# Expert products of a mixture-of-experts stage: sample rows and prompt rows alternated within each feature tile

## The reference, cut to what matters

```python
def expert_choice_ffn(h, w_router, w_gate, w_up, w_down):
    cap = EC_FACTOR * n // N_EXPERTS
    aff = jax.nn.softmax((xt @ w_router).astype(jnp.float32), axis=-1)
    gate, idx = lax.top_k(aff.T, cap)
    xe = jnp.take(xt, idx, axis=0)
    hid = jax.nn.silu(jnp.einsum('ecd,edf->ecf', xe, w_gate)) * jnp.einsum('ecd,edf->ecf', xe, w_up)
    ye = jnp.einsum('ecf,efd->ecd', hid, w_down) * gate[..., None].astype(h.dtype)
```

## Time and profile before

| | |
|---|---|
| median of three runs | 3492.0 us |
| the profiled execution's own time | 3490.68 us |
| its span, first to last instruction | 3488.8 us |
| mean granted TensorE clock | 0.988 of full speed |
| TensorE busy (matmul) | 3366.9 us, 97% |
| VectorE, ScalarE, GpSimd busy | 1302.6, 707.1, 158.1 us |
| DMA traffic | 675.69 MB, mean 194 GB/s |

### The profile page before, as it was taken

How to read it: one execution, slowest core, us unless ns; L and a number is a source line. 1 busy time by engine, 2 the same in 40 slices (tenths; PEclk the granted TensorE clock), 3 DMA queues, 4 the chain that set the end, 5 groups by cost and what they waited for, 6 DMA issues and landing times.

```text
span 3488.8 us, 47739 instructions
## 1 busy us (share of the span) xinstructions
PE 3366.9 (97%) x20879; PEld 1891.6 (54%) x20879; DVE 1302.6 (37%) x2509; ACT 707.1 (20%) x1538; POOL 158.1 (5%) x179
## 2 busy tenths in 40 slices
PE   6999999999999899999989999999999998999998
PEld 4547766765554544434355577677655545444333
DVE  3455443437543311212143544433375423211113
ACT  3131111115332300000021311111153322000001
POOL 1000000000100000000100000000001000000000
PEclk9999999999999899999999999999999999999999
DMA  7343242332232699999952423324412417999997
GB/s 221 103 114 84 66 125 64 103 94 91 81 142 88 227 380 391 396 385 390 385 153 77 134 64 98 93 64 103 109 75 81 165 64 287 383 396 390 395 386 300
DMA packets 218049, 675.69 MB, mean 194 GB/s; under 512 B 9779, under 2 KB 22297, under 8 KB 214257
## 3 DMA queue, kind: packets, MB, share of 16 engines
q1 hardware_dynamic: 198096, 613.97, 49.8%
q0 software_dynamic: 13312, 43.05, 4.8%
q10 hardware_dynamic: 6432, 15.62, 1.2%
HBM read 605.91 MB, written 66.68 MB: 193 GB/s over the span
## 4 chain that ended last, share of the span: by engine, by line
PE 90%; DMA 5%; ACT 3%; DVE 2%; issue 1%; ACTq 0%; DVEq 0%; POOLq 0%
PE unit L842 12%; PE unit L1354 11%; PE unit L790 11%; PE work L1357 9%; PE work L1354 6%; PE unit L854 4%; PE unit L833 3%; PE unit L1226 3%; PE unit L873 3%; PE unit L784 3%; DMA ring<-in_w_e_gate 2%; PE unit L1179 2%; PE work L1044 2%; PE work L1078 2%; PE unit L800 1%; PE work L1144 1%
## 5 line engine op out<-in xcount | busy, mean ns | idle before, releaser
L842 PE MATMUL unit<-hT,ring 128*128 128x512 f32 x1024 | 475.5, 593 | 0.0
L1354 PE MATMUL unit<-ring,arena 128*64 128x512 f32 x1568 | 354.7, 597 | 4.7 <-DMA ring<-in_w_e_gate 3.3
L1357 PE MATMUL work<-ring,arena 128*32 128x256 f32 x4608 | 274.8, 382 | 0.0
L2316 DVE SCALAR_TENSOR_TENSOR arena<-work,arena 32x256 f32<-32x256 f32 x128 | 61.6, 482 | 552.2 <-PE work L1357 550.8
L842 PEld LDWEIGHTS unit<-hT,ring 128*128 128x128 f32 x1024 | 177.9, 191 | 140.6 <-issue 140.6
L1354 PEld LDWEIGHTS unit<-ring,arena 128*64 128x64 f32 x1568 | 109.4, 137 | 225.6 <-issue 214.6
L1357 PEld LDWEIGHTS work<-ring,arena 128*32 128x32 f32 x4608 | 136.8, 109 | 159.5 <-issue 80.6
L790 PE MATMUL unit<-hT,ring 128*128 128x512 f32 x512 | 221.1, 592 | 0.0
L1839 ACT ACTIVATE arena<-work 128x512 f32<-128x512 f32 x32 | 19.1, 597 | 850.0 <-PE work L1371 850.0
L1354 PE MATMUL work<-ring,arena 128*64 128x512 f32 x736 | 166.6, 594 | 2.4 <-ACT arena L1840 2.1
L790 PE MATMUL unit<-arena,ring 128*128 128x512 f32 x384 | 166.8, 592 | 0.0
(11 more groups left out here) (447 smaller groups left out, 4717.6 us busy)
## 6 DMA issues: line engine op xcount, KB each, us to landing
ring<-in_w_e_gate SPq DMA_DIRECT2D x50, 2048.0 KB, 15.1
ring<-in_w_e_up SPq DMA_DIRECT2D x48, 2048.0 KB, 14.2
ring<-in_w_e_down SPq DMA_DIRECT2D x46, 2048.0 KB, 15.7
ring<-in_w_in SPq DMA_DIRECT2D x32, 2048.0 KB, 15.8
ring<-in_w_ada SPq DMA_DIRECT2D x24, 2048.0 KB, 8.8
arena<-in_w_e_down SPq DMA_DIRECT2D x18, 2048.0 KB, 14.9
arena<-in_w_e_up SPq DMA_DIRECT2D x16, 2048.0 KB, 13.7
arena<-in_w_e_gate SPq DMA_DIRECT2D x14, 2048.0 KB, 16.3
```

Of the source, the lines that this page charges most:

```text
L842: last = mm(bank[:, :], w[:, k, m * P:(m + 1) * P], hT[:, k, 0:TS], start=k == 0, stop=k == KD - 1)
L1354: last = mm(big[SLS * c:SLS * c + SLS, :], x, w[:, kk, 512 * c:512 * c + 512], start=k == 0, stop=k == KD - 1)
L1357: last = mm(low[SLOTP * c:SLOTP * c + SLOTP, 0:256], xp, w[:, kk, 256 * c:256 * c + 256], start=k == 0, stop=k == KD - 1)
```

## The change

In five of an expert's six chunks (all but d1) the two runs are gone. Within each feature tile the order is now: the narrow products of quarters 2 and 3, the wide product of half 0, the narrow products of quarters 0 and 1, the wide product of half 1. Chunk d1 keeps a narrow run and then a wide run, as before. Products, operands, banks, waits and the counting of `moe_computed` are the same.

```diff
-                    for wide in ((True, False) if half == 0 else (False, True)):
+
+                    def product(kk, wide, c):
+                        k = 4 * half + kk
+                        if wide:
+                            x = hidT[:, kk, half, :] if kind == "d" else XE[e % 2][:, k, 0:SLS]
+                            return mm(big[SLS * c:SLS * c + SLS, :], x, w[:, kk, 512 * c:512 * c + 512],
+                                      start=k == 0, stop=k == KD - 1)
+                        x = hidTp[:, k % 2, k // 2, :] if kind == "d" else XE[e % 2][:, k, SLS:SLS + SLOTP]
+                        return mm(low[SLOTP * c:SLOTP * c + SLOTP, 0:256], x, w[:, kk, 256 * c:256 * c + 256],
+                                  start=k == 0, stop=k == KD - 1)
+
+                    if part == "d1":
                         for kk in range(4):
...
+                            for c in range(4):
+                                last = product(kk, False, c)
+                        last.then_inc(sig["moe_computed"], 1)
+                        for kk in range(4):
+                            for c in range(2):
+                                last = product(kk, True, c)
+                    else:
+                        for kk in range(4):
+                            for c in range(2):
+                                product(kk, False, 2 - 2 * c)
+                                product(kk, False, 3 - 2 * c)
+                                last = product(kk, True, c)
                     last.then_inc(sig["moe_computed"], 1)
```

More of the change, by code:

```diff
@@ L1346, in expert_chunk @@
                         pe.wait_ge(sig["slots_ready"], 3 * l + 3)
-                    for wide in ((True, False) if half == 0 else (False, True)):
-                        for kk in range(4):
[L1349 to L1360, removed]
+                    def product(kk, wide, c):
[7 more added lines that the diff above has]
+                                  start=k == 0, stop=k == KD - 1)
```

## The result

The changed kernel takes 4628.57 us, the median of 4 runs (4627.2 to 4629.84), against 3492.37 before (4 runs, 3490.94 to 3495.26): a ratio of 1.3253 with a 95% interval of 1.3237 to 1.3268. It is slower by 1136 us. The forecast was 4650, range 4520 to 4780.

The account below looks back on a forecast made before the run. The TensorE was taken to bound the kernel, with DMA close behind. An expert period 36.55 us longer, 32 times, gives 1170 us; less 10 for waits, on 3490.7, that is 4651, stated as 4650, range 4520 to 4780.

Parts of the forecast that it names:

- The column kinds don't share the array: On the TensorE, halves and quarters never stream together; a change of kind drains the array. Forecast chance 0.91, 4650 us.
- The stretches: In each mixed chunk, narrow stretches take 0.57 us and wide ones 1.01, a pair 1.58, a chunk 12.64.
- The edge terms: At stretch edges on the TensorE: entering and leaving cost 0.03 and 0.11 us for narrow, 0.05 and 0.10 for wide.
- Edge price: Cost of a change between halves and quarters on the TensorE: 0.14 us a narrow stretch, 0.15 a wide one.
- The upper bound from the small products of rows 8: Edge costs of 0.22 and 0.19 us, from products of 16 streamed columns, would add 154 us: 4805 us.
- The lower bound: If a stretch's first weights load while the other kind streams, entering costs vanish, 102 us less: 4550 us.
- What else moves: In the expert stages, fewer waits for weights and less backlog take 10 us off, between 4 and 20.
- part of the backlog: Some of the backlog at the end of the first expert stage goes, within the 10 us taken off.
- The rival of the falling clock: With half of the columns idle, the clock drops to 1.2 GHz for half of both expert stages: 5770 us, chance 0.02.
- The rival of strictly ordered starts: In mixed chunks, TensorE passes start strictly in program order without a drain: period 58.5 us, 4285 us, chance 0.02.
- The rival of the shared array: In mixed chunks, halves and quarters stream together, and DMA limits the gain: 3455 to 3490 us, say 3475, chance 0.05.
- The 25 us allowed for layer 1: Most that layer 1's expert stage could shrink if DMA rose from 377 to 395 GB/s.

Follow-up runs that it names:

- e1: The changed kernel's mixed order with each wide product of 64 rows issued as two quarter products of 32 rows: 3493.64 us, ratio 1.0002 to the kernel before.
- e4: The changed kernel, but each mixed chunk runs quarters 2 and 3 for all four feature tiles, then half 0, quarters 0 and 1, half 1: 4367.35 us.
- e7: The kernel before, wide products cut into two quarter products, and three of four expert chunks loading three of four feature tiles: 3459.07 us, ratio 0.9905.
- e6: The kernel before, with three of four expert chunks loading only three of their four feature tiles: 3481.47 us, ratio 0.9974.
- e5: The kernel before, with the wide run doing all four feature tiles of half 0 first, then all of half 1: 3670.41 us.
- e2: The kernel before, runs kept, with each wide product issued as two quarter products of 32 rows: 3495.59 us, ratio 1.0011.

## Why the prediction was right

- **The column kinds don't share the array.** This was the step on which all hung, read from the half that lay idle in rows 6 and 7. It held: the changed kernel's timeline shows it, e1 shows that the kind and nothing else in the order is the cause, and e4 that longer runs don't change it. It was read from a single place in the router's part, and e1 is the run that excludes another cause of the wait there.
- **The stretches.** 0.57 and 1.01 were forecast, 0.56 and 1.00 measured. A chunk takes 12.47 us (1299.74 to 1312.21, where the next one begins) where 12.64 was forecast. The edge terms, taken as differences of rounded rows against 8 x 0.429 and 8 x 0.215, were together 0.02 us too high for a pair of stretches. Times 40 pairs a period that is 0.85 of the 0.86 us between 70.26 and 69.40, which are 27 us over 32 experts. This is the term that made the forecast too high; of the 27 us, 5 are made up for by the waits below.
- **Edge price.** 0.14 and 0.15 a change; 0.134 by e4 against the changed kernel, 0.14 by e7 against e6. The upper bound from the small products of rows 8 (0.22) was far off; their stretches hold their own streaming and pipeline time. The lower bound, entering for nothing, was wrong as well: PEld shows that first weights aren't loaded ahead (1300.30 above).
- **What else moves.** 10 us were taken off for waits for weights. The change of period makes 32 x 35.69 = 1142 us and the span grew by 1136.6, so about 5 came off, near the 4 of the waits alone. The "part of the backlog" doesn't show: the stretch between the stages is 1189.6 us where it was 1187.1. So two misses partly cancelled, 27 us too much for the stretches and 5 too much taken off here, which leaves the 21; both are small beside the 1170.
- **The clock** stayed at 1.00 through the stages, with half of the array idle. The rival of the falling clock did not come about.
- **The rival of strictly ordered starts** (4285) is refuted by e1 and by e5, which would have taken 4025 under it. The rule of the Trainium skill that stands beside it (TensorE: Matmul & The Clock Gate, Part 3, What overlaps and what doesn't), that matmuls start in program order, doesn't hold between column tiles here: in e5 half 1's first pass starts while four passes of half 0, issued before it, are outstanding. The other rule of the Trainium skill, that on mode switching (TensorEngine Tiling (Array Packing), Key Properties), holds between halves and quarters, with 0.134 us and the idle columns as its price.
- **The rival of the shared array** was priced with the right limit. e1 does what it described, with a full array, and it gave 3493.64: its 3475 was too low by 19 us. The DMA engines let 1.5 us through (stages of 544.0 and 542.3 us), and the rest of the execution was 8.3 us longer. The 25 us allowed for layer 1 were too many in any case: they come from a window that runs past the last expert, and up to 3470 us the rate is 383 GB/s, not 377.

## What to carry to other kernels

Products of half and of a quarter of the array's columns never ran side by side here, so group such products in runs, or bring them to one kind: 64 rows as twice 32 cost no time here and made the mixed order as fast as the runs. Before interleaving, look in a timeline for a place where one kind follows another while part of the array is free, and see when the next weight load starts. And a busy TensorE says nothing of how much of its array works (97% before, 98% after): compare passes per microsecond with a full run.

## What the runs showed of the hardware that was not expected

- A column tile's products overtake another tile's queue, but only over a short distance: eight passes in half 0 let half 1 begin at the fifth (e5, and layer 0's gate products of line 1294). Issued in larger blocks, two halves stop overlapping in part, here for 178 us (3670 against 3492).
- Cutting a 64-row product into two of 32 rows doubles its instructions at no cost in streaming: a wide run takes 3.43 us in quarters (e2), exactly 8 x 0.429, where it takes 3.48 to 3.53 in halves between narrow runs.
- The kernel before was balanced closely: 0.86 us less TensorE work in a period of 33.71 (2.6%) shortened the stages by only 2.2 us of 27, since the waits for weights grew from 2.0 and 1.2 to 12.6 and 12.7 us. These are 22 of the 25 that are missing. The rest stays open; it fits that a bar of a wide pass (0.59 us) is drawn 0.16 longer than its pitch (0.43), which hides as much of each wait: 2.5 us over 15 more waits, an estimate.
- In all four kernels in quarters a dip of the clock lies at another place ahead of the first expert than in the six others, though the code there is the same: 4.2 to 4.4 us lost and 1.7 won back. The cause is open. Differences of a few us between whole executions are therefore better read stage by stage.
